# A new order of turning, scoring and weighing in the latent layer of a two-block transformer kernel

## What is computed

```python
def mla_mixer(p, cos, sin, qa_norm, kva_norm, w_q_up, w_kv_up, q_gain, k_gain):
    ...
    q = (rmsnorm(q_lat, qa_norm) @ w_q_up).reshape(b, s, N_MIX_HEADS, MLA_QK_DIM)
    kv = (rmsnorm(kv_lat, kva_norm) @ w_kv_up).reshape(b, s, N_MIX_HEADS, MLA_NOPE_DIM + MLA_V_DIM)
    ...
    q = rmsnorm(q, q_gain).transpose(0, 2, 1, 3) * MLA_QK_DIM ** -0.5
    k = rmsnorm(k, k_gain).transpose(0, 2, 1, 3)
    return from_heads(causal_block_attention(q, k, v.transpose(0, 2, 1, 3)))
...
        x = x + jnp.concatenate([o_mix, o_mem], axis=-1) @ w_out[i]
        x = x + conv_ffn(rmsnorm(x, norm_ffn[i]), ffn_w_up[i], ffn_conv_w[i], ffn_conv_b[i],
                         ffn_w_down[i])
```

## Time and profile before

| | |
|---|---|
| median of three runs | 1295.84 us (1294.86 to 1295.86) |
| the profiled execution | 1295.38 us, of which the span is 1294.0 us |
| PE busy | 1275.6 us, 99% of the span |
| DVE busy | 978.8 us, 76% |
| ACT busy | 700.0 us, 54% |
| POOL busy | 152.5 us, 12% |
| share of PE in the chain that ended last | 89% |
| granted TensorE clock, mean | 1.00 |

### The profile page before, as it was taken

How to read it: one execution, slowest core, us unless ns; L and a number is a source line. 1 busy time by engine, 2 the same in 40 slices (tenths; PEclk the granted TensorE clock), 3 DMA queues, 4 the chain that set the end, 5 groups by cost and what they waited for, 6 DMA issues and landing times.

```text
span 1294.0 us, 19305 instructions
## 1 busy us (share of the span) xinstructions
PE 1275.6 (99%) x7558; PEld 1100.0 (85%) x7558; DVE 978.8 (76%) x1556; ACT 700.0 (54%) x1030; POOL 152.5 (12%) x237
## 2 busy tenths in 40 slices
PE   8999999999999999999999999999999989999999
PEld 8888899889988898888888878888888867888887
DVE  6556587978666747766667877798888887888887
ACT  5445566545545556643334755655554775655553
POOL 8000001000000001200001131000000160000000
PEclk9999999999999999999999999999999999999999
DMA  9632445423555526566665733366665612476662
GB/s 309 197 123 68 165 165 198 165 96 126 185 195 184 207 99 189 152 196 188 188 194 164 228 121 92 99 200 190 196 193 171 222 33 82 132 205 186 189 201 81
DMA packets 219705, 212.67 MB, mean 164 GB/s; under 512 B 7969, under 2 KB 177075, under 8 KB 219616
## 3 DMA queue, kind: packets, MB, share of 16 engines
q1 hardware_dynamic: 215872, 206.25, 51.2%
q0 software_dynamic: 3152, 4.15, 1.0%
q10 hardware_dynamic: 592, 1.05, 0.2%
HBM read 210.25 MB, written 1.05 MB: 163 GB/s over the span
## 4 chain that ended last, share of the span: by engine, by line
PE 89%; DVE 4%; ACT 3%; issue 2%; POOL 1%; DMA 0%; SPq 0%; ACTq 0%; DVEq 0%; POOLq 0%
PE psum_b L2351 9%; PE psum_a L2351 9%; PE psum_a L569 5%; PE psum_a L571 5%; PE psum_a L570 5%; PE psum_c L569 5%; PE psum_b L2354 5%; PE psum_c L570 5%; PE psum_a L2354 5%; PE psum_c L571 5%; PE psum_b L569 4%; PE psum_b L571 4%; PE psum_b L570 4%; PE psum_b L638 2%; PE psum_a L638 2%
## 5 line engine op out<-in xcount | busy, mean ns | idle before, releaser
L508 ACT ACTIVATE w_hi<-raw 128x2048 fp32r<-128x2048 f32 (+3 forms) x231 | 368.7, 1631 | 15.7 <-PE psum_b L2354 4.6
L518 DVE TENSOR_TENSOR w_lo<-raw,w_hi 128x2048 fp32r<-128x2048 f32 (+3 forms) x154 | 339.1, 2216 | 39.5 <-ACT w_hi L508 36.7
L2351 PE MATMUL psum_b<-x,w_hi 128*128 128x512 f32 x528 | 165.6, 395 | 0.0
L2351 PE MATMUL psum_a<-x,w_hi 128*128 128x512 f32 x522 | 164.1, 396 | 0.0
L2354 PEld LDWEIGHTS psum_b<-x,w_lo 128*128 128x128 f32 x528 | 99.2, 188 | 23.2
L531 DVE TENSOR_TENSOR w_lo<-raw,w_hi 128x512 fp32r<-128x512 f32 (+1 forms) x159 | 116.5, 736 | 2.3 <-ACT w_hi L508 2.3
L2354 PEld LDWEIGHTS psum_a<-x,w_lo 128*128 128x128 f32 x522 | 98.1, 188 | 22.8
L2507 ACT ACTIVATE ffn_pre<-ffn_both,cols 128x256 f32<-128x256 f32 x88 | 50.3, 601 | 113.1 <-DVE ffn_both L2519 113.1
L2551 POOL CAST ffn_hidden_hi<-ffn_h 128x256 fp32r<-128x256 f32 x66 | 51.1, 774 | 485.2 <-DVE ffn_h L2538 330.3
L569 PE MATMUL psum_c<-w_hi,ffn_hidden_hi 128*128 128x512 f32 x264 | 103.6, 392 | 0.6 <-DVE ffn_hidden_lo L2543 0.5
L2354 PE MATMUL psum_b<-x,w_lo 128*128 128x256 f32 x528 | 103.7, 278 | 0.0
(11 more groups left out here) (620 smaller groups left out, 2901.8 us busy)
## 6 DMA issues: line engine op xcount, KB each, us to landing
raw<-in_ffn_w_up_dram SPq DMA_DIRECT2D x88, 512.0 KB, 5.1
raw<-in_w_in_dram SPq DMA_DIRECT2D x39, 1024.0 KB, 5.3
raw<-in_w_gu_dram SPq DMA_DIRECT2D x44, 512.0 KB, 5.2
raw<-in_ffn_w_down_dram SPq DMA_DIRECT2D x44, 512.0 KB, 3.3
raw<-in_w_down_dram SPq DMA_DIRECT2D x22, 512.0 KB, 3.4
raw<-in_w_br_ssm_dram SPq DMA_DIRECT2D x8, 1024.0 KB, 5.2
raw<-in_w_xkv_dram SPq DMA_DIRECT2D x8, 1024.0 KB, 5.6
raw<-in_w_out_dram SPq DMA_DIRECT2D x8, 1024.0 KB, 5.2
```

What stands on the lines that cost most here:

```text
L508: act.activation(k.w_hi[:, s, 0:size], k.raw[:, s, 0:size], ACT.Copy).then_inc(*k.rounded.at(*key))
L518: dve.tensor_tensor(k.w_lo[:, s, 0:size], k.raw[:, s, 0:size], k.w_hi[:, s, 0:size].bitcast(F32), ALU.subtract).then_inc(*k.split.at(*key))
L2351: pe.matmul(ps[:, 512 * j:512 * j + 512].rearrange("p (n t) -> p n t", n=2), hi[j], k.X_both[:, :, kt, :], start=kt == 0, stop=False, skip ...
```

## The change

It writes the order anew for attends 2 to 6 on PE, and for the matching stretches of ACT and DVE:

- PE turns pair n + 1 before the probabilities of n, takes one half product step behind the probabilities, then scores n + 1, then weighs n. All of `lat_out` comes in half steps.
- Between attends the steps are dealt out anew. The six steps' worth between attends 3 and 4 used to be four of `psum_a` and two of `psum_b`; now the first step of `psum_b` comes two half steps earlier, at once behind the second half of pair 2's step.
- ACT copies pair n + 1's queries first and the probabilities second; its split of a weight piece stands right behind that copy, in attends 3 to 6. Before, splits stood behind attend 2, 3, 4 and 6.
- DVE copies the keys first, and takes the peaks of n + 1 ahead of the output's low part of n, with at most one third of a piece in front of the peaks.

No instruction is added or removed in the latent layer.

```diff
+def pe_lat_attend_early(k, n, fill):
+
+    pe_lat_turn_pair(k, n + 1)
+    pe_fox_turn_prob(k, n, LatPair)
+    take(fill, 1)
+    pe_lat_scores(k, n + 1)
+    pe_fox_weigh(k, n, LatPair)
+
+
 def pe_mla(k):
...
     take(p, 2)
-    a, b = lat_out(k, 0, 1), lat_out(k, 1, 1)
+    a, b = lat_out(k, 0, 1, True), lat_out(k, 1, 1, True)
     take(p, 1)
-    pe_lat_attend(k, 2)
+    pe_lat_attend_early(k, 2, a)
     take(a, 1)
     pe_lat_rope(k, 1)
+    take(a, 2)
+    pe_lat_attend_early(k, 3, a)
     take(a, 1)
-    pe_lat_attend(k, 3)
-    take(a, 2)
-    take(b, 1)
-    pe_lat_attend(k, 4)
+    take(b, 3)
+    take(a, 1)
+    pe_lat_attend_early(k, 4, a)
     take(b, 1)
     pe_lat_rope(k, 2)
-    take(b, 1)
-    pe_lat_attend(k, 5)
+    take(b, 2)
+    pe_lat_attend_early(k, 5, b)
     take(b, 1)
     a, b = lat_out(k, 0, 0, True), lat_out(k, 1, 0, True)
     take(a, 2)
     take(b, 2)
-    pe_lat_attend(k, 6)
-    take(a, 2)
+    pe_lat_attend_early(k, 6, a)
+    take(a, 1)
     take(b, 2)
     take(a, 2)
...
 def act_lat_attend(k, n):
+    if n < PAIRS - 1:
+        act_lat_turn_pair(k, n + 1)
     act_fox_turn_prob(k, n, LatPair)
     if n < PAIRS - 1:
-        act_lat_turn_pair(k, n + 1)
+        act_split(k, 1)
     act_fox_out(k, n, LatPair)
...
     dve_fox_normalize(k, 3, LatPair)
     dve_lat_rope(k, 1)
     dve_up_keys(k, 2)
+    dve_lat_turn_pair(k, 4)
     dve_fox_turn_prob(k, 3, LatPair)
-    dve_lat_turn_pair(k, 4)
     dve_split_part(k, 1, 3)
+    dve_lat_peaks(k, 4)
     dve_fox_out(k, 3, LatPair)
     dve_split_part(k, 2, 3)
-    dve_lat_peaks(k, 4)
     dve_fox_normalize(k, 4, LatPair)
     dve_split_part(k, 0, 3)
+    dve_lat_turn_pair(k, 5)
     dve_fox_turn_prob(k, 4, LatPair)
...
```

More of the change, by code:

```diff
@@ L3827, in act_mla @@
     act_up_queries(k, 2)
+    act_lat_turn_pair(k, 3)
     act_fox_turn_prob(k, 2, LatPair)
-    act_lat_turn_pair(k, 3)
     act_up_keys(k, 2)
@@ L3832, in act_mla @@
     act_fox_out(k, 2, LatPair)
-    act_split(k, 1)
     act_lat_exp(k, 3)
@@ L3884, in dve_mla @@
     dve_split_part(k, 2, 3)
+    dve_lat_turn_pair(k, 3)
     dve_fox_turn_prob(k, 2, LatPair)
-    dve_lat_turn_pair(k, 3)
     dve_split_part(k, 0, 3)
     dve_up_queries(k, 2)
+    dve_lat_peaks(k, 3)
     dve_up_means(k, 2)
     dve_up_key_means(k, 2)
-    dve_lat_peaks(k, 3)
     dve_fox_out(k, 2, LatPair)
@@ L3895, in dve_mla @@
     dve_up_keys(k, 2)
+    dve_lat_turn_pair(k, 4)
     dve_fox_turn_prob(k, 3, LatPair)
-    dve_lat_turn_pair(k, 4)
     dve_split_part(k, 1, 3)
+    dve_lat_peaks(k, 4)
     dve_fox_out(k, 3, LatPair)
     dve_split_part(k, 2, 3)
-    dve_lat_peaks(k, 4)
     dve_fox_normalize(k, 4, LatPair)
     dve_split_part(k, 0, 3)
+    dve_lat_turn_pair(k, 5)
     dve_fox_turn_prob(k, 4, LatPair)
-    dve_lat_turn_pair(k, 5)
     dve_split_part(k, 1, 3)
+    dve_lat_peaks(k, 5)
     dve_fox_out(k, 4, LatPair)
     dve_split_part(k, 2, 3)
-    dve_lat_peaks(k, 5)
     dve_fox_normalize(k, 5, LatPair)
     dve_lat_rope(k, 2)
+    dve_lat_turn_pair(k, 6)
     dve_fox_turn_prob(k, 5, LatPair)
-    dve_lat_turn_pair(k, 6)
     dve_split_part(k, 0, 3)
+    dve_lat_peaks(k, 6)
+    dve_fox_out(k, 5, LatPair)
     dve_split_part(k, 1, 3)
-    dve_fox_out(k, 5, LatPair)
     dve_split_part(k, 2, 3)
-    dve_lat_peaks(k, 6)
     dve_fox_normalize(k, 6, LatPair)
+    dve_lat_turn_pair(k, 7)
     dve_fox_turn_prob(k, 6, LatPair)
-    dve_lat_turn_pair(k, 7)
     dve_split_part(k, 0, 3)
+    dve_lat_peaks(k, 7)
     dve_fox_out(k, 6, LatPair)
     dve_split_part(k, 1, 3)
-    dve_lat_peaks(k, 7)
     dve_fox_normalize(k, 7, LatPair)
```

## The result

| | before | changed |
|---|---|---|
| median | 1295.01 us (1294.49 to 1295.86, 10 runs) | 1298.45 us (1298.02 to 1299.3, 10 runs) |
| ratio to before | | 1.0026, 95% interval 1.0016 to 1.0036 |
| span of the profiled execution | 1294.0 us | 1296.6 us |
| PE busy | 1275.6 us | 1276.1 us |

The account below looks back on a forecast made before the run. PE was taken to set the pace; two rope waits (+0.84, +1.36) and the later stretches (+0.52, -0.03, -0.04) summed to +2.7 us on 1295.84, giving 1298.5, range 1296.0 to 1300.0.

Parts of the forecast that it names:

- What bounds: Attends 2 to 6: PE sets the pace, busy 40.51 of 42.92 us; a better order can take away 2.4 us.
- the last cut: End of the five counted stretches, attends 2 to 6; the feed-forward part after it was to take as long as before.
- Rope waits: Turnings of pairs 4 and 6 wait for VectorE's rope copy out of the same bank: +0.84 and +1.36 us.
- Thirds: Behind attends 3 and 5, PE waits for VectorE's last weight thirds, 1.34 and 0.74 us; net +0.52 and -0.03.
- rival 1: Weight thirds are hidden and only the rope waits bind: +0.6 us, 1296.4; chance 20%.
- behind s: Counted from s, the start of the next pair's turnings in an attend, in us.
- the sign of being wrong: Wrong if the waits on rope copies and thirds are under 0.5 us, or the part behind 1103 changes over 1 us.
- The attend itself: One attend in the new order: scores at 2.14, weighing done at 5.00 us; 4.31 without its half step, against 4.38.
- The sum: Over attends 2 to 6: 0.84 + 1.36 + 0.52 - 0.03 - 0.04 = 2.65, +2.7 us.
- The half step behind the probabilities: Between the probabilities' turning and the scores, it does not hide VectorE's two copies; 0.07 us gained per attend.
- The drain: VectorE's next instruction waits for an empty pipeline: some 0.5 us before each of four waits, 1300.5; not followed.
- rival 4: PE's clock falls in the pauses of 1.3 to 1.6 us: +4.1 us on top, 1302.6; chance 3%.

Follow-up runs that it names:

- run 2: Changed kernel, with the next group's rope columns turned between scores and weighing in attends 2 and 4, both engines' rope copies moved earlier; 1296.73 us, ratio 1.0012.
- run 1: Changed kernel, with VectorE's last weight thirds behind attends 3, 4 and 5 put ahead of the peaks; 1296.66 us, ratio 1.0012.
- run 8: Changed kernel, with the half product step of attends 2 to 6 moved from in front of the scores to behind the weighing; 1299.72 us, ratio 1.0033.
- run 4: Changed kernel, with ScalarE's four splits put back behind the output copies of attends 2, 3, 4 and 6; 1305.04 us, ratio 1.0086.
- run 7: Kernel before, with only the pair turned ahead of the probabilities in attends 3 and 5, on all three engines; 1299.13 us median, ratio 1.0034.
- run 9: The same kernel as run 7, nothing changed, run once more; 1299.32 us median of nine.
- run 10: Kernel of run 7, plus a half product step between turnings and weighing in attends 3 and 5; 1297.06 us.

## Why the prediction was right

The mechanism and the sign were right, and the time, 1298.5 against 1298.45, also; but deviations hide in that agreement.

- **What bounds.** PE set the pace, its work did not change (1276.1 and 1275.6), and nothing was lost behind the last cut. Right.
- **Rope waits.** Right in place and cause; run 2 takes them away with 1.7 us (1.96 in the stretch). Attends 2 and 4 were counted at 9.18 and 8.96 and took 9.28 and 9.07. The waits themselves are shorter than counted: from when the next matmul was due (0.23 behind the one before, at 1060.68 and 1080.04) PE stood 1.48 and 1.32 instead of 1.76 and 1.54, because it arrived later than counted. The profile lists them as 1.31 and 1.16, since it counts idle time from the modelled end of the matmul before. The hand-over behind the copy was 0.39 and 0.36, as in the earlier trace rows.
- **Thirds.** Right; run 1 takes them away with 1.8 us (1.96 in the stretch), and rival 1 falls. Attend 3's step on `psum_b` went 7.28 behind s instead of 7.03: the third ended at 7.00 (counted 6.93), and PE followed 0.28 later, not 0.10. That is the hand-over whose price was left between 0.10 and 0.36, and I took the wrong end. Attend 5's went at 7.83 (counted 7.81): there the third ended at 7.78, and PE followed 0.05 later. That step issues two waits, attend 3's four; but the score step issues four as well and follows by 0.15, so the number of waits alone does not give the price. Attend 5's wait is also the one that came near the sign of being wrong, a wait under 0.5: it is listed as 0.35 and is 0.50 from when PE was due, where 0.74 was counted, because PE came at 7.33 and not at 7.07.
- **The attend itself.** This term was mis-sized. An attend lasts 5.12 to 5.17 instead of 5.00: the scores follow VectorE's probability copy by 0.15, not 0.10, and the weighing starts 0.43 behind the causal step, not 0.34. And the first product matmul behind a weighing takes 0.10 more than its followers, as in attend 6 of the changed kernel, where five half steps take 3.53 (1095.82 to 1099.35) instead of 3.45:

```profile
1095.02 0.87 PE L2992 MATMUL psum_c<-mla_prob_t,mla_values 128*64 128x256 f32 x8
1095.82 0.50 PE L569 MATMUL psum_a<-w_hi,y 128*128 128x512 f32 x1
1096.15 0.40 PE L570 MATMUL psum_a<-w_lo,y 128*128 128x512 f32 x1
1096.39 0.39 PE L571 MATMUL psum_a<-w_hi,y 128*128 128x512 f32 x1
```

The trace of the kernel before has the same behind its last weighing, so this could have been counted:

```profile
1099.02 0.50 PE L569 MATMUL psum_b<-w_hi,y 128*128 128x512 f32 x1
1099.35 0.39 PE L570 MATMUL psum_b<-w_lo,y 128*128 128x512 f32 x1
```

- **The sum.** Over the five stretches these small terms make +3.55 instead of +2.65. The forecast still met the median because it was added to 1295.84, the median of three earlier runs, while the kernel before gave 1295.01 beside the changed one. So the agreement to 0.05 us is luck: the effect was 3.4, in the range, and above the 2.7 forecast. The last turning's place, 1099.35 where 1099.4 was forecast, is luck too, since this execution began the stretch 0.90 us early and lost 0.90 us more in it than counted. The effect itself lies past the 2.6 us that a measurement can tell from no change.
- **The half step behind the probabilities.** That it gains little was right, but not for all of the reason: each attend was said to win 0.07, but less its half step (0.69) it took some 4.46 against 4.38 before, so it lost about 0.08. And run 8 shows that even without the step behind the probabilities only 1.3 us would be lost.
- **The drain.** The Trainium skill, "VectorE: DVE Perf Modes", section on the drain that can't be avoided, would by the prediction's estimate have given 1300.5; 1298.45 was measured. The rows again have the next instruction before the end of the one before (1063.33 + 0.42 = 1063.75, the next at 1063.67). Whether the pipeline was empty by then no row shows; the count by starts needs nothing more.
- **The clock.** It stayed full in all ten executions of the changed kernel, whose longest pause in the stretch was 1.31 us. But my ground for giving rival 4 only 3% was weak: one pause of 2.6 us at the start without a fall does not show that pauses are harmless. Runs 4, 7 and 9 show falls of 3.4 to 10.2 us behind pauses of 1.2 to 3.0, in some executions. In runs 7 and 9 five of 15 executions, those with a mean clock of 0.996, took 4.4 to 5 us more than the ones with a full clock, and five with 0.999 took 1 to 2.5 us more. The Trainium skill, "TensorE: Matmul & The Clock Gate", section on the oscillation in real kernels, says that gaps between groups of matmuls throttle the clock; runs 4, 7 and 9 agree with it, at 0.50 behind some of their pauses, while other pauses as long in the same profiles, and the profile of the kernel before, did not show it.

## What to carry to other kernels

When a step is pulled forward on the engine that sets the pace, look at what it waits for: here a copy that used to be covered by the turnings ahead of it. The reader's place was changed, and the copy's place in VectorE's queue was not. Waits on separate resources added up in full. The thirds were mended by moving one instruction on VectorE into a gap that its timeline showed; the rope waits by turning the rope columns earlier on PE and moving both engines' copies with them. Only with both mended and the chain of two copies split did the new order pay.

Filling one pause moves idle time to the next fixed wait, so price a filler by the waits left behind it. Where two rows give different hand-overs for an instruction with several waits, carry both through the sum: here it was 0.28 us behind attend 3 and 0.05 behind attend 5. And when the times of one program come in groups, read the mean clock of each execution first: here it told the groups apart.

## What I had not expected of the hardware

- The same program shows groups of times: 1297.7, 1299, and 1302.2 us in run 9, with mean clocks of 1.000, 0.999 and 0.996. The two profiles taken, of the top group in run 7 and of the middle one in run 9, have the granted clock at 0.50 in different places, behind different pauses (2.00; 1.18 with 0.88), while the same or longer pauses (2.03 with 0.88; 2.96 in run 4; 1.99 in run 10) left it full.
- The clock did not fall at a pause's start or end: in run 7 it fell 0.9 us after PE had begun to work again, in run 4 0.7 us after, in run 9 inside a pause of 0.88. Once down, it stayed at 0.50 for 10.2 us in run 7 under a PE that was busy from 1066 on, and for 3.4 us in runs 4 and 9.
- The first product matmul behind a weighing takes 0.33 us to the next (0.50 long) instead of 0.23 (0.39 long).
